# First projection of a twelve-layer block: input in three transfers, first mix in four parts

## The reference

```
xx = time_shift(x) - x                      # the token before, minus the token
xr, xw, xk, xv, xa, xg = [x + xx * mu[n] for n in range(6)]
r, k, v = einsum('nbtc,ncd->nbtd', stack([xr, xk, xv]), w_rkv)
```

## Time and profile before

| | before |
|---|---|
| median of 3 runs | 2022.86 us (2021.9 to 2024.41) |
| the profiled execution, its own time | 2023.78 us |
| its span, first to last instruction | 2022.0 us |
| mean granted TensorE clock | 0.996 |
| PE busy | 1967.4 us (97%) |
| DVE busy | 1275.0 us (63%) |
| ACT busy | 907.3 us (45%) |
| chain that ended last: PE, DVE, ACT | 87%, 8%, 2% |

### The profile page before, as it was taken

The page is one execution under the profiler, slowest core; times in us unless marked ns, Lnnn a source line. Parts: engine busy times, 40 slices in busy tenths (PEclk is TensorE's granted clock), DMA queues, the critical chain, the costliest instruction groups (busy, mean ns, idle before and its releaser), DMA issues.

```text
span 2022.0 us, 30699 instructions
## 1 busy us (share of the span) xinstructions
PE 1967.4 (97%) x12630; PEld 1604.2 (79%) x12630; DVE 1275.0 (63%) x1623; ACT 907.3 (45%) x1284; POOL 160.5 (8%) x198
## 2 busy tenths in 40 slices
PE   7999999999899999999999999999999999999999
PEld 6689788878678878888878678877767888898887
DVE  7874855567765565755767665577886555475554
ACT  4452344434444434444545454434434444444442
POOL 2242100000010010000003011002100000000000
PEclk9999999999999999999999999999999999999999
DMA  8411365646156654565465347653332556454554
GB/s 298 123 52 58 104 215 195 219 152 214 53 175 206 224 176 169 175 188 187 166 192 189 109 134 225 200 185 128 105 125 93 181 195 218 159 194 156 187 168 155
DMA packets 93044, 335.97 MB, mean 166 GB/s; under 512 B 11230, under 2 KB 11364, under 8 KB 92623
## 3 DMA queue, kind: packets, MB, share of 16 engines
q1 hardware_dynamic: 85824, 311.62, 45.9%
q0 software_dynamic: 7120, 22.95, 4.2%
HBM read 332.43 MB, written 1.05 MB: 165 GB/s over the span
## 4 chain that ended last, share of the span: by engine, by line
PE 87%; DVE 8%; ACT 2%; POOL 1%; issue 1%; DMA 0%; SPq 0%; DVEq 0%; ACTq 0%; POOLq 0%
PE acc L420 43%; PE acc L506 20%; PE acc L477 8%; DVE w_lo L1660 2%; PE acc L978 2%; PE aux L899 1%; PE aux L526 1%; PE aux L683 1%; POOL rstd L2507 1%; PE aux L966 1%; DVE w_spare_lo L1660 1%; PE aux L934 1%; PE acc L670 1%; ACT w_hi L1238 1%; POOL rstd L2510 1%
## 5 line engine op out<-in xcount | busy, mean ns | idle before, releaser
L1660 DVE TENSOR_TENSOR w_lo<-w_raw,w_hi 128x1024 fp32r<-128x1024 f32 x552 | 670.3, 1225 | 527.7 <-ACT w_hi L1238 524.1
L1238 ACT ACTIVATE w_hi<-w_raw 128x1024 fp32r<-128x1024 f32 x552 | 580.0, 1059 | 714.7 <-PE acc L420 438.3
L420 PE MATMUL acc<-w_hi,operand_hi 128*128 128x512 f32 x1232 | 488.8, 397 | 14.5 <-DVE operand_lo L1843 12.3
L420 PE MATMUL acc<-w_hi,operand_lo 128*128 128x512 f32 x1232 | 481.8, 391 | 0.0
L420 PE MATMUL acc<-w_lo,operand_hi 128*128 128x512 f32 x1232 | 481.2, 391 | 0.0
L420 PEld LDWEIGHTS acc<-w_hi,operand_hi 128*128 128x128 f32 x1232 | 231.9, 188 | 63.3 <-DVE operand_lo L1843 12.1
L420 PEld LDWEIGHTS acc<-w_hi,operand_lo 128*128 128x128 f32 x1232 | 231.7, 188 | 49.1
L420 PEld LDWEIGHTS acc<-w_lo,operand_hi 128*128 128x128 f32 x1232 | 232.2, 188 | 46.8 <-issue 0.5
L506 PE MATMUL acc<-w_hi,hidden_hi 128*128 128x512 f32 x528 | 207.9, 394 | 0.0
L506 PE MATMUL acc<-w_hi,hidden_lo 128*128 128x512 f32 x528 | 205.9, 390 | 0.0
L506 PE MATMUL acc<-w_lo,hidden_hi 128*128 128x512 f32 x528 | 205.6, 389 | 0.0
(11 more groups left out here) (485 smaller groups left out, 2432.5 us busy)
## 6 DMA issues: line engine op xcount, KB each, us to landing
w_raw<-in_weights SPq DMA_DIRECT2D x552, 512.0 KB, 3.5
w_spare_raw<-in_weights SPq DMA_DIRECT2D x36, 512.0 KB, 5.2
ln_gain<-in_gains POOLq DMA_DIRECT2D x7, 512.0 KB, 4.5
bias_at<-in_rpb POOLq DMA_DIRECT2D x12, 256.0 KB, 4.7
ln_gain<-in_ln_g POOLq DMA_DIRECT2D x4, 512.0 KB, 4.2
ln_bias<-in_ln_b POOLq DMA_DIRECT2D x4, 512.0 KB, 5.6
vec_rw<-in_vec POOLq DMA_DIRECT2D x3, 512.0 KB, 5.4
l_rw<-in_lora SPq DMA_DIRECT2D x1, 1152.0 KB, 10.5
```

What stands on the lines that cost most here:

```text
L420: mm = pe.matmul(acc[:, 2 * pair + t, :], (ah, al)[x][:, kt, t * P:(t + 1) * P], weight(w, q + i)[:, kk * 512:(kk + 1) * 512], start=(kt = ...
L1238: act.activation(weight(0, q), raw_of(q), ACT.Copy).then_inc(hi_of(q)[0], 1)
L1660: dve.tensor_tensor(weight(1, q), raw_of(q), weight(0, q).bitcast(F32), ALU.subtract).then_inc(lo_of(q)[0], 1)
```

## The change

The input comes in three transfers (channel tiles 0 and 1; 2 and 3; 4 to 7), the second behind quarter 0 and the third behind quarter 1 on SP's queue. The first mix is no longer x + xx·mu from the differences, but an own share x·(1 − mu), made by ACT with the column `OWN` as scale, plus a shifted share added by DVE in place (255 elements, from the token before). It is made in four parts of two channel tiles, each with its own high part, low part and wait on PE. The differences, which the other five mixes still use, are made after the four parts. Two semaphores that had a single use are merged into others (`causal_in` into `masks_in`, `rev2_in` into `hyena_in`), and some counts follow.

```
@@ SP @@
         sp.dma_start(MU[:], A["mu"]).then_inc(m["x_in"], 16)
-        sp.dma_start(XT[:, 0:4, :], A["xT"][:, 0:4, :]).then_inc(m["x_in"], 16)
-        sp.dma_start(XT[:, 4:KT, :], A["xT"][:, 4:KT, :]).then_inc(m["x2_in"], 16)
+        sp.dma_start(XT[:, 0:2, :], A["xT"][:, 0:2, :]).then_inc(m["x_in"], 16)
...
+                if n == 0 and k == 0:
+                    sp.dma_start(XT[:, 2:4, :], A["xT"][:, 2:4, :]).then_inc(m["x2_in"], 16)
+                if n == 0 and k == 1:
+                    sp.dma_start(XT[:, 4:KT, :], A["xT"][:, 4:KT, :]).then_inc(m["x3_in"], 16)
@@ PE @@
             for i in range(4):
-                if operand_half and i % 2 == 0:
+                if operand_half and i in parts:
                     operand_half()
...
+                    block_tokens(q + 4 * b, b, operand_half=None if b else mix_half, parts=range(4) if first else (0, 2))
@@ ACT @@
-            for h in range(2):
-                split(q + h)
-                mix_hi(0, h)
+            def own_share(p):
+
+                for k in (2 * p, 2 * p + 1):
+                    last = act.activation(MIX[0][:, k, :], XT[:, k, :], ACT.Copy, scale=OWN[:, k:k + 1])
+                last.then_inc(m["own_ready"], 1)
+
+            act.wait_ge(m["x_in"], due(m["x_in"], 32))
+            act.wait_ge(m["mix_f_ready"], due(m["mix_f_ready"]))
+            own_share(0)
+            split(q)
+            act.wait_ge(m["x2_in"], due(m["x2_in"], 16))
+            own_share(1)
+            mix_hi(0, slice(0, 2))
+            split(q + 1)
+            act.wait_ge(m["x3_in"], due(m["x3_in"], 16))
+            own_share(2)
+            mix_hi(0, slice(2, 4))
             split(q + 2)
+            own_share(3)
+            mix_hi(0, slice(4, 6))
             split(q + 3)
+            mix_hi(0, slice(6, 8))
@@ DVE @@
+            def add_shifted(p):
+
+                dve.wait_ge(m["own_ready"], due(m["own_ready"]))
+                for k in (2 * p, 2 * p + 1):
+                    last = dve.scalar_tensor_tensor(out=MIX[0][:, k, 1:SEQ], in0=XT[:, k, 0:SEQ - 1], scalar=MU[:, 0, k:k + 1], in1=MIX[0][:, k, 1:SEQ],
+                                                    op0=ALU.mult, op1=ALU.add)
+                last.then_inc(m["mix_f_ready"], 1)
+
             dve.wait_ge(m["x_in"], due(m["x_in"], 32))
-            differences(0)
-            mix(0, 0, 0)
-            dve.wait_ge(m["x2_in"], due(m["x2_in"], 16))
-            differences(1)
-            split(q)
-            half_lo(0, 0)
-            mix(0, 0, 1)
-            split(q + 1)
-            half_lo(0, 1)
-            dve.wait_ge(m["mix_ready"], due(m["mix_ready"], 2))
-            split(q + 2)
-            split(q + 3)
+            dve.tensor_scalar(OWN, MU[:, 0, :], -1.0, 1.0, ALU.mult, ALU.add).then_inc(m["mix_f_ready"], 1)
+            for p in range(4):
+                add_shifted(p)
+                split(q + p)
+                part_lo(0, slice(2 * p, 2 * p + 2))
+            dve.wait_ge(m["mix_ready"], due(m["mix_ready"], 4))
+            for h in range(2):
+                differences(h)
             mix_all(2, 1)
             ahead(q, 2)
```

More of the change, by code:

```diff
@@ L173, in program @@
     XT, XX = IC[:].rearrange("p t (k n) -> p (t k) n", n=SEQ), DEC[:].rearrange("p t (k n) -> p (t k) n", n=SEQ)
+    OWN = stat[:, 0:KT]
     MIX = [TMP[:].rearrange("p t (k n) -> p (t k) n", n=SEQ), KK[:].rearrange("p t (k n) -> p (t k) n", n=SEQ)]
@@ L220, in program @@
     m = {n: sem(n) for n in (
-        "x_in", "x2_in", "rwkv_in", "vec_in", "gn_in", "consts_in", "res_in", "ln_in", "attend_in", "causal_in", "bias_in", "bias_masked", "bias_hi_ready", "ident_r_set", "hyena_in", "rev2_in", "fw3_built",
+        "x_in", "x2_in", "x3_in", "rwkv_in", "vec_in", "gn_in", "consts_in", "res_in", "ln_in", "attend_in", "bias_in", "bias_masked", "bias_hi_ready", "ident_r_set", "hyena_in", "fw3_built",
         "spare_full", "spare_hi", "spare_lo", "spare_used", "constants_set", "presets", "bias_ready",
         "gain_in", "half_done", "residual_done", "ln_done", "square_ready", "eps_added", "ms_ready", "rstd_ready", "token_ready", "turned", "hi_ready", "operand_ready", "dve_step",
-        "mix_f_ready", "mix_ready", "rkv_done", "lora1_ready", "lora_mid", "lora2_ready", "lora_out", "cum_ready", "span_ready",
+        "own_ready", "mix_f_ready", "mix_ready", "rkv_done", "lora1_ready", "lora_mid", "lora2_ready", "lora_out", "cum_ready", "span_ready",
         "exp_ready", "k_and_bonus", "scaled_ready",
@@ L425, in part_tokens, with block_tokens @@
             return mm
-        def block_tokens(q, pair, at=None, operand_half=None, after={}, beside=None):
+        def block_tokens(q, pair, at=None, operand_half=None, parts=(0, 2), after={}, beside=None):
             for i in range(4):
-                if operand_half and i % 2 == 0:
+                if operand_half and i in parts:
                     operand_half()
@@ L542, in mixed @@
             def mixed(mixes):
-                pe.wait_ge(m["mix_f_ready"], due(m["mix_f_ready"], 2 * mixes))
+                pe.wait_ge(m["mix_f_ready"], due(m["mix_f_ready"], mixes))
             def pair(q, first=False):
@@ L549, in pair @@
                         pe.wait_ge(m["rkv_done"], due(m["rkv_done"]))
-                    block_tokens(q + 4 * b, b, operand_half=None if b else mix_half)
+                    block_tokens(q + 4 * b, b, operand_half=None if b else mix_half, parts=range(4) if first else (0, 2))
             pair(q, True)
             pe.wait_ge(m["rwkv_in"], due(m["rwkv_in"], 16))
-            mixed(3)
+            mixed(1 + 4 + 2 * 2)
             lora1(0, LORA, aux[:, 0], MIX[0]).then_inc(m["lora1_ready"], 1)
             pair(q + 8)
-            mixed(2)
+            mixed(2 * 2)
             lora1(LORA, 2 * LORA, aux[:, 1], MIX[0]).then_inc(m["lora1_ready"], 1)
@@ L599, in rwkv @@
             pe.wait_ge(m["rkv_done"], due(m["rkv_done"]))
-            mixed(1)
+            mixed(2)
             lora1(2 * LORA, 2 * LORA + P, acc[:, 2], MIX[0])
@@ L1315, in copy_out, with mix_hi @@
                 last.then_inc(m["rkv_done"], 1)
-            def mix_hi(src, h):
+            def mix_hi(src, ks):
                 act.wait_ge(m["mix_f_ready"], due(m["mix_f_ready"]))
-                ks = slice(4 * h, 4 * h + 4)
                 act.activation(ah[:, ks, :], MIX[src][:, ks, :], ACT.Copy).then_inc(m["hi_ready"], 1)
@@ L1329, in project_out @@
                         for h in range(2):
-                            mix_hi(1, h)
+                            mix_hi(1, slice(4 * h, 4 * h + 4))
                     copy_out(dst, c, q + 4 * c + 3)
-            for h in range(2):
-                split(q + h)
-                mix_hi(0, h)
+            def own_share(p):
[13 more added lines that the diff above has]
+            mix_hi(0, slice(2, 4))
             split(q + 2)
+            own_share(3)
+            mix_hi(0, slice(4, 6))
             split(q + 3)
+            mix_hi(0, slice(6, 8))
             act.wait_ge(m["constants_set"], CONSTANTS["halves"])
@@ L1838, in mix_all, with part_lo @@
                     mix(n, dst, h)
-            def half_lo(src, h):
+            def part_lo(src, ks):
                 dve.wait_ge(m["hi_ready"], due(m["hi_ready"]))
-                ks = slice(4 * h, 4 * h + 4)
                 dve.tensor_tensor(al[:, ks, :], MIX[src][:, ks, :], ah[:, ks, :].bitcast(F32), ALU.subtract).then_inc(m["mix_ready"], 1)
@@ L1846, in mix_lo @@
                 for h in range(2):
-                    half_lo(src, h)
+                    part_lo(src, slice(4 * h, 4 * h + 4))
                 dve.wait_ge(m["mix_ready"], due(m["mix_ready"], 2))
-            dve.wait_ge(m["x_in"], due(m["x_in"], 32))
-            differences(0)
-            mix(0, 0, 0)
-            dve.wait_ge(m["x2_in"], due(m["x2_in"], 16))
-            differences(1)
-            split(q)
-            half_lo(0, 0)
-            mix(0, 0, 1)
-            split(q + 1)
-            half_lo(0, 1)
-            dve.wait_ge(m["mix_ready"], due(m["mix_ready"], 2))
-            split(q + 2)
-            split(q + 3)
+            def add_shifted(p):
[4 more added lines that the diff above has]
+                last.then_inc(m["mix_f_ready"], 1)
+            dve.wait_ge(m["x_in"], due(m["x_in"], 32))
+            dve.tensor_scalar(OWN, MU[:, 0, :], -1.0, 1.0, ALU.mult, ALU.add).then_inc(m["mix_f_ready"], 1)
[6 more added lines that the diff above has]
+                differences(h)
             mix_all(2, 1)
@@ L2469, in inside_block @@
                     products(1, 2)
-            dve.wait_ge(m["rev2_in"], due(m["rev2_in"], 32))
+            dve.wait_ge(m["hyena_in"], due(m["hyena_in"], 32))
             even_odd_weights(1)
@@ L2614, in load_moba @@
             load(ROPE[:], A["rope"], m["attend_in"])
-            load(CSTAGE[:], A["causal"], m["causal_in"])
-            pool.wait_ge(m["causal_in"], due(m["causal_in"], 16))
+            load(CSTAGE[:], A["causal"], m["masks_in"])
```

(3 more changed lines are left out.)

## The result

The change made the kernel slower: median 2027.45 us (14 runs, 2023.83 to 2030.48) against 2023.5 us (14 runs of the kernel before beside them, 2020.74 to 2026.02). The ratio is 1.0019, 95% interval 1.0012 to 1.0026, so 3.95 us were lost where a gain of 1.1 us was forecast; the time lies above the forecast range of 2019.8 to 2024.6. The profiled execution took 2027.52 us (span 2025.7, granted clock 0.996).

What follows compares the result with a forecast made beforehand. PE, busy 97% of the span, was taken to bound the kernel. Starting 2.8 us earlier but waiting 1.7 us ahead of quarter 4, it would keep 1.1 us: 2022.86 − 1.1 = 2021.8 us, range 2019.8 to 2024.6.

Steps and rivals of the forecast that it cites:

- Further on: After quarter 6: later requests, 1.3 us later, are covered by some 7 us, so the 1.1 us gain reaches the end.
- DVE's lateness: DVE's chain up to quarters 4 and 6: falls back 1.3 us against its earlier times, out of a slack of 2.4.
- the own share: Scaled copies on ACT for the first mix: two 128x256 copies, 0.49 us each, 0.89 us for the pair.
- the low part: A 128x512 low part on DVE: 0.688 us, against 1.22 for today's half.
- The first input part lands at 4.7, the quarter at 6.05: First transfers: with 1.37 us per 512 KB, first input part at 4.7 us, first weight quarter at 6.05.
- The hole ahead of quarter 4: First projection: PE waits 1.7 us for DVE, begins quarter 4 at 23.97; 1.1 of 2.8 us gain are left.
- The parts: First mix in four parts: parts 1 to 3 are ready before PE wants them, so PE does not wait.
- Rival 1: Start to quarter 4: PE keeps more of the lead, gaining 1.8 us (2021.1) or 2.8 (2020.0); chance 0.10.
- Rival 4: Start: slow scaled copies on ACT keep PE's start near 12 us; gain 0.7 us, 2022.2; chance within the forecast's 0.55.
- Rival 2: First weight quarter lands late: at 6.75 gives 2022.5 us, at 8.32 gives 2024.0; chance 0.14.
- Rival 3: Ahead of quarter 4: the new hole drops TensorE's clock, price 1.7 us, giving 2023.5; chance 0.13.
- the prediction's own signs of being wrong: PE finds quarter 4 ready, matmuls behind the hole 0.43 us apart, or stages past 60 us moving by another shift.

Runs made afterwards that it cites:

- kernel 2: The changed kernel with the second mix's high and low parts ahead of quarter 11's split on ACT and DVE: 2024.36 us, ratio 1.0002.
- kernel 3: The changed kernel with quarters 4 and 5 split between and behind the differences on DVE, 6 and 7 behind one mix: 2024.08 us, ratio 1.0004.
- kernel 6: The kernel before with the two differences made a second time behind quarter 3, making DVE late: 2029.37 us, ratio 1.0029.
- kernel 1: The changed kernel without ACT's own wait for the input, so the table load has no wait in front: 2030.19 us, ratio 1.0033.
- kernel 8: The kernel before with only DVE's order changed: quarters 4 and 5 split ahead of the later mixes, 6 and 7 behind one: 2024.27 us, ratio 1.0000.
- kernel 7: Kernel 4 with the input in two halves, the second behind quarter 0, and high part 0 ahead of own share 1: 2021.91 us, ratio 0.9988.
- kernel 5: The changed kernel with two lora loads (520 KB and 512 KB) issued ahead of `ident` and `taps` on GpSimd: 2025.5 us, ratio 1.0009.
- kernel 4: The changed kernel with the edits of kernels 1, 2 and 3 together: 2021.93 us, ratio 0.9993.

## Why the prediction was wrong

**The step that failed** is "Further on": "Quarter 8 is asked for when quarter 4 is split [...] so 1.3 us more is covered by some 7", and from it "So the 1.1 us go through to the end". It followed one request that DVE's lateness moves, and asked only when PE wants that quarter. Quarter 11, three requests on, has next to no cover on ACT: in the kernel before it lands at 35.46 and ACT takes it at 36.19, so 0.7 us. And what stands behind it on ACT is not work for quarter 11 but the operand of the next projection, which PE wants at once. Even the forecast's own 1.3 us exceed the 0.7. They also put the request behind the lora load, whose issue is paced by PE: by an estimate from the rows before, 29.26 + 1.3 = 30.56 for the request and 30.95 − 1.1 = 29.85 for the load. The runs show this step from three sides: kernel 2 takes the operand out of the queue, kernel 3 makes the request early, kernel 6 makes it late in the kernel before. In place of a gain that goes through they showed a gap of 3.91 us ahead of the second projection, and 1.45 us more behind it.

**DVE's lateness, 1.3 us in the sum, was 2.8** (quarter 7 split at 32.0, not 29.2). Of the chain on DVE itself nothing was off: 14.16 us from the first low part (10.09) to the split of quarter 4 (24.25), 14.18 by the working; a part takes 2.53, not 2.55; the own share 0.89 to 0.91, where 0.89 was taken; the low part 0.68 to 0.69, as rows 6 had it. (Of the table that gave the prediction 0.594, in the Trainium skill, VectorE: DVE Perf Modes, the TRN2 errata, the same section says that its row comes out too low for a single operation.) The whole error is in what comes before, 10.09 rather than 8.53:

- The table load is missing from the sum. In the kernel before it ran at 0.73, before any wait. With two waits ahead of ACT's first instruction it starts at 5.59, behind one of them. Kernel 1 gives its price: 0.70 of the 1.56 us. There the landing of the second input part (7.91) takes over on the chain, since ACT makes own share 1 ahead of high part 0. The Trainium skill (ScalarE: Activation LUTs, What ACT_TABLE_LOAD costs) gives about 1283 ns for it, as the trace (1.28 us) does.
- "The first input part lands at 4.7, the quarter at 6.05": they landed at 5.3 and 6.65, and the second input part at 8.0, not 6.75, which is the other 0.86. The working scaled a transfer's time with its bytes; every landing followed the one before it at about 1.3 us all the same, parts of 256 KB and quarters alike. The fit that the prediction took from the Trainium skill (DMA: Bandwidth & Descriptors, Anatomy of one DMA) is given there for loads issued by GpSimd; these are SP's, so it was no price for them.

**The hole ahead of quarter 4** came where it was put and was released by the low weights on DVE, as forecast. From 24.53, where the quarter before ends at 0.23 a matmul, it was 1.0 us, not 1.7 (0.84 in the brackets, which count from the modelled end of the last matmul), since PE started later and ran 13 matmuls at the slow rate, not ten. But quarter 4 began at 25.53, not 23.97. So the forecast gain was already gone by the start that was mis-sized; the step that failed turned a place 0.63 us behind at the lora matmuls into one 5.93 behind at the next ones.

**The parts.** PE did not wait inside the four parts, as forecast.

**The rivals.** Rivals 1 and 4 did not come: the lead was not kept, and ACT's scaled copies took what was taken for them. Rival 2 (quarter 0 late) was partly true, 0.6 us, short of the 7.1 at which it was to decide. Rival 3's mechanism appeared at another place: the hole ahead of quarter 4 left the clock at full, the one of 3.91 us did not, and cost 1.45 us (23.47 against 22.02 for the 96 matmuls). The forecast's 1.7 for such a fall was a fair size. The rest of the 5.93, 4.49, is the 0.63 that PE was behind already, and the gap, to 0.05 us. Of the prediction's own signs of being wrong only the last came: the stages past 60 us moved by other than the shift of the start.

**The end.** Of the 5.93 us at 67.70 only 3.74 are left at the end of the profiled executions. 0.8 of it came back in the recurrence between 131 and 241 us; that stage's length, whose instructions none of these edits touches, lies between 108.7 and 111.5 us over all ten kernels, so 0.8 is within what it varies by. Where the rest goes was not traced to a step. Over the kernels the median goes with PE's place near 66 us: kernels 1 and 6 and the change, 5.5 to 6.4 us behind there, are slower than the kernel before by an interval that excludes no change, kernels 2, 3 and 8, within 0.5 us, are the same, and kernel 7, 2.65 us ahead, is faster; kernel 5, 1.9 behind, and kernel 4, 1.5 ahead, lie between and can't be told from no change. Each place is that of the one profiled execution, with its own luck at the slow rate; for kernels 2 and 4 that execution took 2029.73 and 2026.35 us, 5.4 and 4.4 above their medians.

## What to carry to other kernels

When an engine is made later, list every request that its instructions release, and for each look not at who uses the data but at what stands behind the instruction that waits for it; the smallest margin decides, not the first one met. A margin of a transfer is to be taken with the other queues' traffic at the new time. And where ACT's first instruction gets a second wait, look at where its table load now stands.

## What the runs showed of the hardware

- Transfers of 256 KB (128 rows of 2 KB) at the start of this kernel took as long as those of 512 KB (128 rows of 4 KB): for the first one, issued at 1.18, 4.1 to 4.4 us in six kernels against 4.1 to 4.4 in four, and about 1.3 us from each landing to the next for both.
- A 512 KB quarter issued some 0.5 us behind the 520 KB lora load on the other queue flew 8.0 to 8.7 us (the change and kernels 1, 2 and 6), and 7.5 us issued 0.15 ahead of it (kernel 7). It flew 5.8 to 6.4 us where that load came 1.1 us or more later (the kernel before, kernels 3, 4 and 8) or had landed (kernel 5). That the DMA engines take turns between the queues that have work is stated in the Trainium skill (DMA: Bandwidth & Descriptors, Queues, rings and completion order), and these flights agree with it.
- From its first matmul PE ran 7 to 14 matmuls at the slow rate, 11, 13 and 14 of them in three kernels that start it at 10.81 to 10.85.
- In the first 70 us, holes of PE of 3.29, 3.91 and 3.94 us were followed by a stretch at 1.2 GHz (in kernel 1 from the fourth matmul on, in the others at once); holes of 0.73 to 2.01 us with the clock at full before them were not.
